# Two late RMSNorms of a hybrid decoder step: sums of squares in one column per 64 tokens, and a quarter of the weighting on GpSimd

## The reference, cut to what matters

```
def rmsnorm(x, g):
    xf = x.astype(jnp.float32)
    y = xf * lax.rsqrt(jnp.mean(xf * xf, axis=-1, keepdims=True) + EPS)
    return (y * g.astype(jnp.float32)).astype(x.dtype)
...
    n2 = rmsnorm(x, norm_ffn)
    g_up = n2 @ w_ffn_gate
...
    x = x + (jax.nn.silu(g_conv) * (n2 @ w_ffn_up)) @ w_ffn_down
    n3 = rmsnorm(x, norm_ple)
    x = x + (pe.astype(x.dtype) @ w_ple) * jax.nn.sigmoid(n3 @ w_ple_gate)
```

## Time and profile before

| | us |
|---|---|
| median of 3 runs | 2874.43 (2872.31 to 2874.89) |
| the profiled execution, its own time | 2872.35 |
| its span, first to last instruction | 2870.6 |
| TensorE (PE) busy | 2842.4, 99% of the span |
| VectorE (DVE), ScalarE (ACT), GpSimd (POOL) busy | 1742.9, 1207.9, 290.4 |

### The profile page before, as it was taken

How to read it: one execution, slowest core, us unless ns; L and a number is a source line. 1 busy time by engine, 2 the same in 40 slices (tenths; PEclk the granted TensorE clock), 3 DMA queues, 4 the chain that set the end, 5 groups by cost and what they waited for, 6 DMA issues and landing times.

```text
span 2870.6 us, 52927 instructions
## 1 busy us (share of the span) xinstructions
PE 2842.4 (99%) x19824; PEld 2790.4 (97%) x19824; DVE 1742.9 (61%) x2218; ACT 1207.9 (42%) x1809; POOL 290.4 (10%) x456
## 2 busy tenths in 40 slices
PE   8999999999999999999999999999999999999998
PEld 7899999999999999999999999999999999999998
DVE  7776776877768655555455555655555555555564
ACT  5554554554545433333333335433333333333453
POOL 3221221212212100000000001000000000000100
PEclk9999999999999999999999999999999999999999
DMA  7666565565656565555555555555555555445463
GB/s 206 175 184 189 158 192 158 171 200 148 199 160 172 166 175 156 158 145 151 146 147 147 146 149 159 141 150 151 151 148 147 153 148 151 147 146 151 142 178 111
DMA packets 753984, 457.33 MB, mean 159 GB/s; under 512 B 14697, under 2 KB 747297, under 8 KB 753585
## 3 DMA queue, kind: packets, MB, share of 16 engines
q1 hardware_dynamic: 679705, 414.21, 50.8%
q10 hardware_dynamic: 73528, 39.39, 4.8%
q0 software_dynamic: 672, 2.66, 0.2%
HBM read 430.73 MB, written 25.47 MB: 159 GB/s over the span
## 4 chain that ended last, share of the span: by engine, by line
PE 95%; DVE 0%; ACT 0%; issue 0%; ACTq 0%; DVEq 0%
PE ps L1661 30%; PE ps L1663 30%; PE ps L1662 30%; PE ps L1880 1%; PE ps L2033 1%; PE ps L1890 1%; PE ps L2048 1%; PE ps L2044 0%; PE ps L1785 0%; PE ps L1795 0%; PE ps L1786 0%; PE ps L2006 0%; PE ps L2019 0%; PE ps L2011 0%; PE ps L2057 0%
## 5 line engine op out<-in xcount | busy, mean ns | idle before, releaser
L1661 PE MATMUL ps<-n_hi,whi 128*128 128x320 f32 x4144 | 1287.3, 311 | 3.5 <-issue 2.7
L1663 PE MATMUL ps<-n_hi,wlo 128*128 128x320 f32 x4144 | 1281.1, 309 | 0.0
L1662 PE MATMUL ps<-n_lo,whi 128*128 128x320 f32 x4144 | 1281.0, 309 | 0.0
L1053 DVE TENSOR_TENSOR wlo<-raw,whi 128x1024 fp32r<-128x1024 f32 x746 | 924.0, 1249 | 486.4 <-ACT whi L687 485.4
L687 ACT ACTIVATE whi<-raw 128x1024 fp32r<-128x1024 f32 x746 | 784.0, 1057 | 845.6 <-PE ps L1663 782.4
L1661 PEld LDWEIGHTS ps<-n_hi,whi 128*128 128x128 f32 x4144 | 778.5, 188 | 6.9 <-issue 4.1
L1662 PEld LDWEIGHTS ps<-n_lo,whi 128*128 128x128 f32 x4144 | 778.5, 188 | 0.6
L1663 PEld LDWEIGHTS ps<-n_hi,wlo 128*128 128x128 f32 x4144 | 778.3, 188 | 0.0
L1661 PE MATMUL ps<-c_hi,whi 128*128 128x320 f32 x1728 | 534.7, 309 | 0.5 <-DVE c_lo L1167 0.5
L1663 PE MATMUL ps<-c_hi,wlo 128*128 128x320 f32 x1728 | 534.0, 309 | 0.0
L1662 PE MATMUL ps<-c_lo,whi 128*128 128x320 f32 x1728 | 533.9, 309 | 0.0
(11 more groups left out here) (301 smaller groups left out, 1805.2 us busy)
## 6 DMA issues: line engine op xcount, KB each, us to landing
raw<-in_w_in SPq DMA_DIRECT2D x322, 512.0 KB, 5.1
raw<-in_w_ffn_gate SPq DMA_DIRECT2D x88, 512.0 KB, 4.8
raw<-in_w_ffn_up SPq DMA_DIRECT2D x88, 512.0 KB, 5.0
raw<-in_w_ffn_down SPq DMA_DIRECT2D x88, 512.0 KB, 4.1
raw<-in_w_ssm_out SPq DMA_DIRECT2D x64, 512.0 KB, 4.1
h<-in_state_ssm ACTq DMA_DIRECT2D x32, 512.0 KB, 5.2
out_ssm_sample<-hn ACTq DMA_DIRECT2D x32, 512.0 KB, 4.3
raw<-in_w_sc_out SPq DMA_DIRECT2D x32, 512.0 KB, 4.0
```

The costliest lines, as they stand in the source:

```text
L1053: tt(wlo[slot][:], raw[slot][:], whi[slot][:].bitcast(F32), SUB).then_inc(lo_split, 1)
L1661: mm(out, w_h, x_h, start=first, stop=False)
L1662: mm(out, w_h, x_l, start=False, stop=False)
L1663: return mm(out, w_l, x_h, start=False, stop=last)
```

## The change

The sum of squares is formed with the squares as the stationary operand, 64 tokens at a time, and one column of ones as the moving one: five 64-token blocks and two channel tiles give ten float32 matmuls for each call of `add_squares`, whose results are columns of 64 partitions: columns 0 to 4 of the bank for the sum so far, 8 to 12 for the last pair. VectorE works on 64x5 in place of 128x320: scale and add, a second scale and add for the other five columns, and the reciprocal into `inv_ms`. A new function `spread` puts the result back on 128 partitions by five float32 matmuls (a column of `inv_ms`, repeated 128 times, as stationary operand, the 64x64 identity as the moving one); it stands ahead of the last tile of the first `w_ple` piece. ScalarE takes the root straight from that bank. TensorE's wait ahead of tile 1 of the second piece is now for the root.

ScalarE's `gain_early` keeps twelve of the sixteen tiles. The last four (`sig_a`, `scv`) are written by GpSimd at its step "rms", two multiplications of 128x640 with the weights broadcast along the tokens; they come behind GpSimd's last addition into `sq_sum` and wait for the seventh and the eighth output addition. VectorE's `scaled(3)` waits for these.

```
@@ ScalarE, rms
-                gain_early(n, 6)
-                gain_early(n, 7)
-                act.wait_ge(var_ready, n)
-                activate(rstd[:], var[:], ACT.Sqrt).then_inc(rstd_ready, 1)
+                act.wait_ge(rstd_spread, n)
+                activate(rstd[:], ps[:, RMS_BANK[n], 0:NT], ACT.Sqrt).then_inc(rstd_ready, 1)
@@ VectorE, mean_square
-                own(ts(var[:], ps[:, RMS_BANK[n], 0:NT], 1.0 / DM, EPS, MUL, ADD))
-                v.reciprocal(var[:], var[:]).then_inc(var_ready, 1)
+                own(ts(inv_ms[:], ps[0:NS, RMS_BANK[n], 0:5], 1.0 / DM, EPS, MUL, ADD))
+                own(stt(inv_ms[:], ps[0:NS, RMS_BANK[n], 8:13], 1.0 / DM, inv_ms[:], MUL, ADD))
+                v.reciprocal(inv_ms[:], inv_ms[:]).then_inc(var_ready, 1)
@@ VectorE, scaled
-                    dve.wait_ge(gained_early, 16 * (n - 2) + 4 * h + 4)
+                    if h < 3:
+                        dve.wait_ge(gained_early, 12 * (n - 2) + 4 * h + 4)
+                    else:
+                        dve.wait_ge(gained_late, 2 * (n - 1))
@@ GpSimd, tasks
-                elif kind == "rms" and j == 3:
-                    pool.wait_ge(sq_summed, SUMS[3])
-                    g_.memset(sq_sum[:], 0.0).then_inc(sq_added, 1)
+                elif kind == "rms":
+                    for i, dst in ((6, sig_a[:]), (7, scv[:, :, 0:NT])):
+                        pool.wait_ge(out_added, OUTS_BEFORE[j] - 8 + i + 1)
+                        k = PARAMS[f"g{j}"][0] + 2 * i
+                        g_.tensor_tensor(dst, xt[:, 2 * i:2 * i + 2, :],
+                                         ptab[:, k:k + 2].unsqueeze(2).broadcast_to([P, 2, NT]), ALU.mult
+                                         ).then_inc(gained_late, 1)
+                    if j == 3:
+                        pool.wait_ge(sq_summed, SUMS[3])
+                        g_.memset(sq_sum[:], 0.0).then_inc(sq_added, 1)
@@ TensorE, add_squares and spread
-                for t in range(2):
-                    last = mm(ps[:, RMS_BANK[n], 0:NT], ones[:], part[:, t, :],
-                              start=t == 0 and not last_piece, stop=t == 1 and last_piece)
+                first = 8 if last_piece else 0
+                for c in range(NT // NS):
+                    for t in range(2):
+                        last = mm(ps[0:NS, RMS_BANK[n], first + c:first + c + 1], part[:, t, c * NS:(c + 1) * NS],
+                                  ones[:, 0:1], start=t == 0, stop=t == 1)
...
+            def spread(n):
+
+                pe.wait_ge(var_ready, n)
+                for c in range(NT // NS):
+                    last = mm(ps[:, RMS_BANK[n], c * NS:(c + 1) * NS], inv_ms[:, c:c + 1].broadcast_to([NS, P]),
+                              ident[0:NS, 0:NS], start=True, stop=True)
+                last.then_inc(rstd_spread, 1)
@@ TensorE, the ple pieces
                         if j % 2 and t == 1:
-                            pe.wait_ge(var_ready, 2 + j // 2)
+                            pe.wait_ge(rstd_ready, 2 + j // 2)
+                        if j % 2 == 0 and t == 3:
+                            spread(2 + j // 2)
```

More of the change, by code:

```diff
@@ L296, in hybrid_decoder @@
         rms_t = s2("rms_t", [P, 3])
+        inv_ms = s2("inv_ms", [NS, NT // NS])
         post.close()
@@ L350, in hybrid_decoder @@
         xg_a, xg_v, gained_early = sem("xg_a"), sem("xg_v"), sem("gained_early")
+        gained_late = sem("gained_late")
         sq_summed, var_ready, ysum_ready = sem("sq_summed"), sem("var_ready"), sem("ysum_ready")
@@ L724, in gain_early @@
                 for k in (2 * i, 2 * i + 1):
-                    dst = (nt[:, k // 4, k % 4, :] if k < 8 else chunk[:, k - 8, :] if k < 12 else
-                           sig_a[:, k - 12, :] if k < 14 else scv[:, k - 14, 0:NT])
+                    dst = nt[:, k // 4, k % 4, :] if k < 8 else chunk[:, k - 8, :]
                     activate(dst, xt[:, k, :], copy, scale=ptab[:, gain + k:gain + k + 1]).then_inc(gained_early, 1)
```

## The result

The median went from 2872.61 us (16 runs, 2871.48 to 2875.50) to 2880.72 us (16 runs, 2878.21 to 2885.14): a ratio of 1.0026, 95% interval 1.0019 to 1.0032. That is slower by 0.2 to 0.3%, +8.1 us between the medians and +7.6 between the means, where I had forecast +1.58 us (2876.0, from 2874.43 as the median of three runs of before) and no change that can be measured. The profiled execution of after took 2878.21 us with a span of 2876.5, against 2872.35 and 2870.6 for before.

What follows compares the result with a forecast made beforehand. The prediction took TensorE's stream of matmuls as the bound. Stop removed -2.35, added TensorE work +3.08, GpSimd-VectorE collision +0.85 gave +1.58 us: median 2876.0 us from 2874.43, range 2872.2 to 2879.5.

Steps and rivals of the forecast that it cites:

- the clock falls: Rival: narrow products at both norms halve TensorE's granted clock for stretches; 2880.2 us or more, chance 0.06.
- the likeliest case: The forecast itself: stop gone, more TensorE work, GpSimd and VectorE colliding at the norms; +1.58 us, chance 0.57.
- TensorE's extra work: Narrow sums and `spread` less the removed wide sums: 1.54 us more per norm, 3.08 in all.
- The narrow slot: Time per narrow float32 record on TensorE: 0.0625 us in the nearest row, taken as 0.065.
- The collision: GpSimd's new multiplications delay VectorE, so TensorE waits ahead of `spread`: 0.75 us at first norm, 0.1 at second, +0.85.
- The lower end of the range: 2872.2 us, said to come from the cheaper-products case with the runs' own scatter, 2.1 below the median.
- the stop of 2.35 us: TensorE's standing still ahead of both norms' first matmuls, 1.10 + 1.25 us, claimed to go altogether.
- the turns of GpSimd and VectorE: At a late norm their instructions alternate whole, 4.68 us from GpSimd's end until VectorE is free for the sums.
- the three small instructions: VectorE's 64x5 instructions replacing its two 128x320 passes behind the sums: 0.56 us together.
- the narrow products are not cheaper between full ones: Denies a rival: weight loads hide under neighbouring wide products, narrow ones cost half; 2873.4 us, chance 0.17.
- the last rival: Narrow records on TensorE don't overlap, 0.2 us each, 5.4 us more per norm; 2887 us, chance 0.04.
- the stop doesn't stay: Denies a rival: the stop ahead of the norm's matmuls stays, or the collision is dearer; 2878 to 2880, chance 0.13.

Runs made afterwards that it cites:

- e3: The changed kernel with 48 columns of ones as moving operand in place of one; 2875.02 us, ratio 1.0006 to the kernel before.
- e5: The changed kernel with 16 columns of ones as moving operand in place of one; 2875.44 us, ratio 1.0009 to the kernel before.
- e8: The changed kernel with 48 columns of ones and no weighting moved to GpSimd; 2875.01 us, ratio 1.0009 to the kernel before.
- e1: The kernel before with only GpSimd's two multiplications and the twelve-tile `gain_early`, sums unchanged; 2876.46 us, ratio 1.0009.
- e4: The changed kernel with its narrow products taken apart, one channel pair ahead of each full product; 2889.97 us, ratio 1.0063 to the kernel before.
- e2: The changed kernel with the last quarter's weighting back on ScalarE; 2880.91 us, ratio 1.0022 to the kernel before.
- e6: The kernel before with the narrow products added as unused extra work beside its 320-column sums; 2876.17 us, ratio 1.0009.

## Why the prediction failed

**The step that failed** is the chance given to the rival "the clock falls", and the sentence that held it down: "here each 1.3 us of narrow work is followed by six full products". The profile of after refutes it: six full products stood behind the first group of narrow sums, and from the second group on the clock was at half for 10.4 us. The row that the rival went by, was a stretch where TensorE also stood still; in after its busy time stays at 1.00 of the stretch throughout. So the busy share doesn't tell the two cases apart: in e3, e5 and e8 it is as high, and the same records in the same places with 16 or 48 columns leave the clock at 1.00. The Trainium skill, "TensorE: Matmul & The Clock Gate", part 1 ("What's actually happening"), has the array throttled unless it is kept busy; the trace agrees with it in e1, where the half clock follows 1.86 us of standing still, but in after the engine's own busy time shows nothing missing.

**Its price** was near the truth. I had said that a stretch costs half its length, which is 5.2 us of 10.4; against the undisturbed second norm the first took 15.96 - 11.39 = 4.6 more. With 11.39 for each undisturbed norm the three profiles of after lose 4.6, 6.2 and 7.7 us to the clock, most of their distance to before.

**The sum** of the likeliest case comes near where the clock doesn't fall: e3, e5 and e8, which are the change at full clock but for the wider products, have norm stretches 2.35 to 2.42 us over before (means +1.8, +2.7 and +2.2), against my +1.58. But two of its terms are off and partly cancel, so that it comes so near is in part luck. TensorE's extra work was 3.08 for both norms. At the second norm of after it is 11.39 less the 9.19 that the earlier trace rows leave without the stop (10.37 - 1.18), 2.20 in place of 1.54. The narrow slot was right; what was left out is the change from full products to narrow and back, some 0.1 us on each side of a group (2735.34 to 2735.58 is 0.24 where a slot has 0.147), and `spread` takes 1.26 in place of 1.10. e4 confirms that the changes cost by multiplying them. The collision was 0.85 (0.80 by the prediction's own starts) and is nearly nothing: the turns came as forecast, but the slower sections bring TensorE to `spread` later, so that at full clock it hardly waits. At the second norm of after the row of `spread` comes 0.24 behind the last product, as at the other changes; at the first norm it is 0.28 in e3 and 0.33 in e5, so the wait is 0.1 at most. The lower end of the range, too, is not what its terms give (2873.4 - 2.1 = 2871.3); that has no part in the miss.

**Right** were: the stop of 2.35 us goes (no idle ahead of the norm's matmuls in the profiles of after); 0.0625 a record; the turns of GpSimd and VectorE, 4.5 us against 4.68; 0.56 for the three small instructions. The other rivals are settled so: the narrow products are not cheaper between full ones, they are dearer; no record takes the 0.2 us of the last rival at full clock; and the stop doesn't stay.

**Open** is why the clock fell at one norm only in one profile of after and at both in two others and in e2, and why in one of them it came later at the first norm, in the row of `spread`. The instructions are the same; what the fall waits for was not tried. That the wide sums beside the narrow ones kept the clock of e6 at 1.00 is argued, too, and was not tried by itself.

## What to carry to other kernels

Before matmuls with few moving columns replace wide ones on the engine that sets the end, ask what they do to the granted clock, and read it in the stretch behind them: here a busy share of 1.00 stood beside a granted clock of 0.51. If such products are needed, try them with more columns, since 48 cost 0.05 us per twenty records more than one and kept the clock here, and keep them in few groups, because each change to them and each change back cost some 0.1 us. The stop at the end of the chain was better removed by a shorter chain (one instruction on the engine that reads the bank) than by more work on the engine that waits.

## What the runs showed of the hardware

Twenty float32 records in a row cost 1.25 us with 1 column and 1.30 with 48: the columns are nearly hidden. The granted clock behind them was 1.00 with 48 and 16; with one it was 0.50 to 0.57 at one norm or at both in the profiles of after and e2, and 1.00 at the second norm of one of them and in e6, where wide sums stand beside them. Two instructions of VectorE back to back, 1.2 us each, don't keep GpSimd out: both reading SBUF, they took 4.28 and 4.29 us, because a GpSimd instruction that stood waiting came in between. The Trainium skill, "SBUF — State Buffer", section "Who interferes with whom", says that a VectorE instruction with two inputs in SBUF contends with a GpSimd instruction that reads SBUF; the rows agree, GpSimd's second taking 2.25 where the first took 1.27. Here the two engines alternated. ScalarE's reciprocal root of 128x320 from PSUM took 0.53 us, VectorE's reciprocal of the same size on SBUF 2.15.
